# An fp32 kernel of two transformer blocks: the place of the first additions of each part, the size of the weight sums, and the first attention blocks behind a feed-forward layer

## The chip, the cores and the metric

The kernel runs on one core of one Trainium2 chip. The time is device microseconds of the slowest core, here the only one. The kernel before takes 1590.38 us, the median of three runs (1589.19 to 1590.43).

## The reference

A sequence of 512 tokens of width 1,024 in float32 goes through two blocks. The second has two layers, and the change lies in it: the feed-forward layers, and the attention between them (the first block and the first layer's mixer are left out here).

```python
def squared_relu_mlp(n, w_up, w_down):          # w_up 1024 x 4096, w_down 4096 x 1024
    return jnp.square(jax.nn.relu(n @ w_up)) @ w_down

def mixer_c(n, w_in, gq, gk, w_out):            # 8 heads of 128
    q, k, v = _split(n @ w_in, (C_WIDTH, C_WIDTH, C_WIDTH))
    q = rmsnorm_2(q.reshape(bsz, s_len, N_HEADS_C, HEAD_DIM), gq)
    k = rmsnorm_2(k.reshape(bsz, s_len, N_HEADS_C, HEAD_DIM), gk)
    return stick_breaking(q, k, v).reshape(bsz, s_len, C_WIDTH) @ w_out

# stick_breaking, for every head, z = q @ k.T / sqrt(128), only keys before the token:
#   lo = log_sigmoid(-z);  rc = cumsum of lo from the right
#   a = exp(log_sigmoid(z) + rc - lo);  out = a @ v

for layer in range(2):
    n = rmsnorm_2(h, g_mix[layer])
    h = h + (mixer_ab(n, ...) if layer == 0 else mixer_c(n, ...))
    h = h + squared_relu_mlp(rmsnorm_2(h, g_ffn[layer]), w_up[layer], w_down[layer])
```

## The kernel before, in words

**Arithmetic.** Float32 products are made of three matmuls on a high part and a remainder of each operand (`three`, L612 to L614): high x high, remainder x high, high x remainder. A tile of weights has 128 partitions x 2,048 columns (1 MB; eight chunks of the contraction by 256 output columns). SyncE issues its DMA into one of two buffers `raw`, ScalarE copies it rounded into `wh` (the high part), and VectorE subtracts that from `raw` into `wl` (the remainder). The activations are split in the same way. Each engine's order is written out by hand, in one function for each engine; semaphores join them.

**Projection blocks.** A block is 8 chunks x 3 matmuls that fill one PSUM bank. Two banks, G0 and G1, take the blocks in turn, so a block can begin only when the one two before it has been copied out (`take_block`). The other six banks are C0, C1, C2, AV, ST and SX.

**A feed-forward layer** (`layer(f)` in each engine's function) has four parts. A part makes 8 up blocks into `wide` (relu, square, on VectorE L2913 and ScalarE), and multiplies them by its share of `w_down` in seven products of half the size instead of eight, on sums of quarters. The sums of quarters of the weights are GpSimd's: `weight_sum` (L2073), four in a part (t3 = b22 - b12, b12 = b12 - b11, b11 = b22 - b12, b21 = b21 - b11), each in two halves of four pieces of 256 columns; a semaphore is raised after each half. GpSimd also makes the sums of quarters of the values, `pair_sums` (L2078). The last weight sum of a part waits for VectorE's second remainder of product 1 (`half_lo`).

**A product** (`product`, L1222; its matmuls are L1231 to L1233) is four chunks x two banks x three matmuls. Products 0, 2, 4 and 6 use banks C0 and C1, 3 and 5 use C2 and AV, and 1 uses ST and SX. For each, ScalarE rounds the weight quarter in two halves, and VectorE makes two remainders of 1,024 columns (`half_of(i, a)`, L2876). VectorE also adds the finished banks to the accumulator in `wide` (`add_up`, L2896), two instructions for each product, and makes the remainders of pairs of values (`second_pair`, L2876 with 128x512). Since products 0 and 2 share their banks, TensorE waits ahead of product 2 for `acc_added` of product 0, and inside it for the remainders of the last pair of values and of the weights. VectorE's order there is: half_of(1, 0), half_of(1, 1), second_pair(3), half_of(2, 0), add_up(0), half_of(2, 1).

**The end of the first feed-forward layer.** After its last product the sums are transposed (`turn_back`, eight times four transposes, L1259) into banks of the list `BACK` and added to h (`final_add`, L2866). h is then rounded and its remainder formed, chunk by chunk (`feed` on ScalarE, L1395 and L1401; `low` on VectorE, L2232), while GpSimd adds up the squares (`add_squares`, L1955) and splits the sum (L2138). TensorE sums that over the partitions (`norm_stat(4)`, L677 and L678), and ScalarE and VectorE form the root (`rsqrt`, L1379 to L1381; `newton`, L2201 and L2202).

**The attention of the second layer** (`attention_group("stick", g, ...)`) has four groups of two heads. A group projects six blocks from three weight tiles: 0 to 3 (query and key of both heads), 4 and 5 (values). Each of 0 to 3 is squared and summed over the partitions (`head_stat`, the same L677 and L678) for its own norm. TensorE does the scores (`do_scores`, L698), the running sums and turns of the weights (`do_turns`, L712) and their products of the heads of the group before between the blocks of the group at hand; ScalarE and VectorE form the weights (`weights`). In the first group nothing is left of a group before. There blocks 0 and 1 are made side by side, chunk by chunk (`first_stick_blocks`), since the chunks of h come one after another, with the last four `turn_back` after the second chunk; then comes `norm_stat(4)`, then blocks 2 and 3, each of which needs a G bank that was copied out with the norm's root.

## Time and profile before

| | before |
|---|---|
| median of three runs | 1590.38 us (1589.19 to 1590.43) |
| the profiled execution, its own time | 1590.34 us |
| its span | 1588.5 us |
| ScalarE busy | 726.9 us, 46% |
| DMA, mean over the span | 91 GB/s, queue 1 at 26.4% of 16 engines |
| up projections, first line L612, 816 matmuls of 128x512 | 326.1 us, 400 ns each |
| remainders of weights, L2876, 102 of 128x1024 | 172.9 us, 1,707 ns each |

The span is the time from the first to the last instruction; 1.8 us of the profiled time lie around it. Busy times say how much of the span an engine worked; engines run beside each other. The duration of a matmul includes its way through the pipeline: one begins some 0.23 us after the one before, while each lasts 0.39. GB/s and clock are given over the span in 40 slices, and TensorE's granted clock is in the highest tenth in each of them.

### The profile page before, as it was taken

The numbers are of one execution on the slowest core, as the hardware profiler recorded it, in microseconds if no ns is written. First come the engines' busy times: TensorE is split into PE (matmuls) and PEld (weight loads), VectorE is DVE, ScalarE is ACT, GpSimd is POOL, SyncE is SP. The second block draws the span as 40 slices with busy tenths as digits, with TensorE's granted clock in tenths as the row PEclk, the third lists the DMA queues.
The fourth block names the chain that finished last, engine by engine and source line by source line (L and its number), as shares of the span: only waits on it lengthen the run. The fifth ranks groups of instructions, "written<-read, shape, count | busy, mean of one in ns | idle before, by whom it ended". The sixth has DMA issues, their size and how long they took to land.

```text
span 1588.5 us, 20549 instructions
## 1 busy us (share of the span) xinstructions
PE 1562.5 (98%) x7570; PEld 1280.4 (81%) x7570; DVE 1033.2 (65%) x1343; ACT 726.9 (46%) x1084; POOL 672.2 (42%) x666
## 2 busy tenths in 40 slices
PE   9999999999999999999999999899999999999999
PEld 7888787887778898888888888688886888888887
DVE  7424554675678977458484848868777557575847
ACT  6323423324245655434343435567765453444433
POOL 0002120114346443385656657423333484847574
PEclk9999999999999999999999999999999999999999
DMA  7232222232211221323233231222121314141321
GB/s 244 80 106 80 79 79 79 95 106 89 98 53 57 91 79 55 132 80 130 83 106 106 85 128 30 77 80 80 54 80 40 146 53 159 53 159 54 135 78 54
DMA packets 25731, 145.07 MB, mean 91 GB/s; under 512 B 3936, under 2 KB 5680, under 8 KB 9264
## 3 DMA queue, kind: packets, MB, share of 16 engines
q1 hardware_dynamic: 25648, 143.95, 26.4%
q8 instruction: 53, 0.87, 0.2%
q14 instruction: 30, 0.25, 0.1%
HBM read 141.84 MB, written 2.10 MB: 91 GB/s over the span
## 4 chain that ended last, share of the span: by engine, by line
PE 76%; POOL 11%; DVE 9%; ACT 2%; issue 2%; DVEq 0%; ACTq 0%; POOLq 0%
PE ps_G L612 17%; PE ps_G L614 17%; PE ps_G L613 17%; POOL wide L2078 4%; PE ps_C L1231 4%; PE ps_C L1233 4%; PE ps_C L1232 4%; POOL tabs L2073 2%; POOL raw L2073 2%; POOL mixed_buffers L2078 1%; PE ps_C L698 1%; PE ps_AV L1074 1%; PE ps_AV L1232 1%; PE ps_AV L1233 1%; PE ps_AV L1231 1%
## 5 line engine op out<-in xcount | busy, mean ns | idle before, releaser
L612 PE MATMUL ps_G<-ch,wh 128*128 128x512 f32 x816 | 326.1, 400 | 1.7 <-DVE cl L2232 1.6
L613 PE MATMUL ps_G<-cl,wh 128*128 128x512 f32 x816 | 318.4, 390 | 0.0
L614 PE MATMUL ps_G<-ch,wl 128*128 128x512 f32 x816 | 318.3, 390 | 0.0
L612 PE MATMUL ps_G<-nh,wh 128*128 128x512 f32 x504 | 199.7, 396 | 0.4 <-DVE h L2440 0.2
L614 PE MATMUL ps_G<-nh,wl 128*128 128x512 f32 x504 | 196.3, 390 | 0.0
L613 PE MATMUL ps_G<-nl,wh 128*128 128x512 f32 x504 | 196.2, 389 | 0.0
L2876 DVE TENSOR_TENSOR wl<-raw,wh 128x1024 fp32r<-128x1024 f32 (+1 forms) x102 | 172.9, 1707 | 33.2 <-ACT wh L1837 25.1
L612 PEld LDWEIGHTS ps_G<-ch,wh 128*128 128x128 f32 x816 | 153.6, 188 | 42.4 <-issue 7.4
L613 PEld LDWEIGHTS ps_G<-cl,wh 128*128 128x128 f32 x816 | 153.7, 188 | 34.0 <-issue 3.1
L614 PEld LDWEIGHTS ps_G<-ch,wl 128*128 128x128 f32 x816 | 153.6, 188 | 32.4
L2167 DVE TENSOR_TENSOR wl<-raw,wh 128x2048 fp32r<-128x2048 f32 x46 | 107.4, 2334 | 65.2 <-ACT wh L1357 62.1
L1357 ACT ACTIVATE wh<-raw 128x2048 fp32r<-128x2048 f32 x60 | 114.4, 1907 | 69.8 <-PE ps_G L614 69.8
L1881 ACT ACTIVATE wide<-tmp 128x512 f32<-128x512 f32 x64 | 40.5, 632 | 219.1 <-DVE tmp L2913 219.0
L1231 PE MATMUL ps_C<-wh,nh 128*128 128x512 f32 x320 | 125.6, 392 | 4.7 <-DVE wide L2896 4.7
L1233 PE MATMUL ps_C<-wh,nl 128*128 128x512 f32 x320 | 124.6, 389 | 0.0
L1232 PE MATMUL ps_C<-wl,nh 128*128 128x512 f32 x320 | 124.6, 389 | 0.0
L2876 DVE TENSOR_TENSOR nl<-wide,nh 128x512 fp32r<-128x512 f32 (+1 forms) x80 | 68.7, 866 | 85.3 <-ACT nh L1885 46.5
L612 PE MATMUL ps_G<-wh,ch 128*128 128x256 f32 (+1 forms) x400 | 119.1, 298 | 0.0
L614 PE MATMUL ps_G<-wh,cl 128*128 128x256 f32 (+1 forms) x400 | 115.6, 289 | 0.0
L613 PE MATMUL ps_G<-wl,ch 128*128 128x256 f32 (+1 forms) x400 | 115.5, 289 | 0.0
L612 PEld LDWEIGHTS ps_G<-nh,wh 128*128 128x128 f32 x504 | 94.6, 188 | 25.3 <-issue 5.5
L614 PEld LDWEIGHTS ps_G<-nh,wl 128*128 128x128 f32 x504 | 94.6, 188 | 20.1
(426 smaller groups left out, 3150.0 us busy)
## 6 DMA issues: line engine op xcount, KB each, us to landing
raw<-wst SPq DMA_DIRECT2D x96, 1024.0 KB, 5.0
raw<-quart_d SPq DMA_DIRECT2D x16, 1024.0 KB, 4.9
tabs<-quart_d SPq DMA_DIRECT2D x8, 1024.0 KB, 6.9
mixed_buffers<-quart_d SPq DMA_DIRECT2D x8, 1024.0 KB, 5.1
raw<-wst SPq DMA_DIRECT2D x8, 256.0 KB, 6.3
out<-wide SPq DMA_DIRECT2D x8, 256.0 KB, 2.0
h<-xT SPq DMA_DIRECT2D x7, 256.0 KB, 6.5
raw<-wst SPq DMA_DIRECT2D x2, 512.0 KB, 5.5
```

What stands on the lines that cost most here:

```text
L612: mm(o, ah, bh, start=first, stop=False)
L613: mm(o, ah, bl, start=False, stop=False)
L614: return mm(o, al, bh, start=False, stop=last)
L1231: mm(o, ah, bh[:, c, :], start=fresh and c == 0, stop=False, skip_group_check=True)
L1232: mm(o, ah, bl[:, c, :], start=False, stop=False, skip_group_check=True)
L1233: return mm(o, al, bh[:, c, :], start=False, stop=c == 3, skip_group_check=True)
L1357: A(wh[s][:], raw[s][:], ACT.Copy).then_inc(w_hi, 1)
L1881: A(wide[:, k, :], tmp[:, k % 2, :], ACT.Square).then_inc(hid_set, 1)
L2073: ins = g.tensor_tensor(dst[:, w], x[:, w], y[:, w], ALU.subtract)
L2078: g.tensor_tensor(dst, x, y, op).then_inc(value_sums, 1)
L2167: v.tensor_tensor(wl[s][:], raw[s][:], wh[s][:].bitcast(F), ALU.subtract).then_inc(w_lo, 1)
L2876: return tt(lo, x, hi.bitcast(F), ALU.subtract)
```

## The change

Three things change.

First, in every part of both feed-forward layers VectorE adds product 0 to the accumulator (`add_up(0)`) right after the two weight remainders of product 1, ahead of the pair's remainder and the first remainder of product 2, behind which it stood.

Second, `weight_sum` on GpSimd makes each half with one instruction of 1,024 columns instead of four of 256. The semaphore is raised as often as before.

Third, the way from the first feed-forward layer into the attention. ScalarE and VectorE make the high part and the remainder of the second weight tile of the attention already within the end of the layer, between the chunks of h. TensorE works on four blocks: 0 and 1 in the G banks as before, 2 and 3 in banks C0 and C1 (`EARLY`), all on the chunks that are there; the eight turn_back use C2, AV, SX and ST twice. `norm_stat(4)` stands behind chunk 5 of blocks 0 and 1, and the rest of the four blocks comes behind it. The first group's order on ScalarE and VectorE is rewritten to this, blocks 4 and 5 take over the G banks from blocks 2 and 3's places in the count (`after=k - 2`), and the row sum of block 3 (`head_stat`) moves into the second group, behind the scores and block 0.

```diff
@@ end of the first feed-forward layer, TensorE
-        BACK = ("C2", "AV", "SX", "ST", "C0", "C1", "C2", "AV")
+        BACK = ("C2", "AV", "SX", "ST", "C2", "AV", "SX", "ST")
+        EARLY = {2: "C0", 3: "C1"}
...
+                st, end = Step("stick", 0), Part(0, 3)
+                def some(blocks, chunks):
+                    for c in chunks:
+                        pe.wait_ge(n_lo, 8 * LO_OF[4] + c + 1)
+                        for k in blocks:
+                            o, s, col = ps[EARLY.get(k, f"G{st.bank(k)}")], st.slot(k // 2), k % 2 * P
+                            ins = three(o[:], wh[s][:, c, col:col + P], wl[s][:, c, col:col + P], mh[:, c, :], ml[:, c, :],
+                                        c == 0, c == KC - 1)
+                            if c == KC - 1:
+                                give_block(ins, st, k)
                 need_tile(st, 0)
-                for c in range(KC):
-                    pe.wait_ge(n_lo, 8 * LO_OF[4] + c + 1)
-                    for k in range(2):
-                        project_some(st, k, mh, ml, [c], c == 0, c == KC - 1)
-                    if c == 1:
-                        pe.wait_ge(acc_added, Part(0, 3).added(6))
-                        for f in range(4, KC):
-                            pe.wait_ge(h_new, f - 3)
-                            turn_back(f, BACK[f])
+                take_block(st, 0)
+                take_block(st, 1)
+                some((0, 1), range(3))
+                pe.wait_ge(acc_added, end.added(6))
+                for f in range(4, KC):
+                    pe.wait_ge(h_new, f - 3)
+                    turn_back(f, BACK[f])
+                need_tile(st, 1)
+                some((2, 3), range(3))
+                some((0, 1, 2, 3), (3,))
+                some((0, 1), (4, 5))
                 norm_stat(4)
+                some((0, 1), (6, 7))
+                some((2, 3), range(4, KC))
@@ attention_group, TensorE
+                if name == "stick" and g == 1:
+                    stands(pe, before, 2)
+                    stands(pe, before, 3)
...
-                if blocks01 is not None:
-                    blocks01()
-                else:
-                    block_(0, 0, 0)
-                    block_(1, 0, P)
+                if first_blocks is not None:
+                    first_blocks()
+                    head_stat(("qk", qk0))
+                    block_(4, 2, 0)
+                    head_stat(("qk", qk0 + 1))
+                    block_(5, 2, P)
+                    head_stat(("qk", qk0 + 2))
+                    return
+                block_(0, 0, 0)
+                if name == "stick" and g == 1:
+                    head_stat(("qk", qk0 - 1))
+                block_(1, 0, P)
@@ attention_group, ScalarE, the first group of four
+                if g == 0:
+                    rsqrt(("norm", 4))
+                    evac_qk(0, 0)
+                    evac_qk(1, 1)
+                    split(st, 1)
+                    rsqrt(("qk", qk0))
+                    act.wait_ge(rt_set, 2)
+                    evac_qk(2, 2)
+                    values_out(wide[:, 12, :], st, 4, 0)
+                    rsqrt(("qk", qk0 + 1))
+                    split(st, 2)
+                    evac_qk(3, 3)
+                    rsqrt(("qk", qk0 + 2))
+                    values_out(wide[:, 13, :], st, 5, 1)
+                    rsqrt(("qk", qk0 + 3))
+                    return
@@ end of the first feed-forward layer, ScalarE, behind feed(4, c, c % 2)
+                    if c == 1:
+                        act.wait_ge(raw_full[1 - t % 2], st.tile_use(5) * 16 + 16)
+                        free(6, 0)
+                        A(wh[1 - s][:, 0:4, :], raw[1 - t % 2][:, 0:4, :], ACT.Copy).then_inc(second_hi, 1)
+                    if c == 2:
+                        free(6, 1)
+                        A(wh[1 - s][:, 4:8, :], raw[1 - t % 2][:, 4:8, :], ACT.Copy).then_inc(w_hi, 1)
@@ layer(f), GpSimd
-                            for n in range(4 * a, 4 * a + 4):
-                                w = slice(n * TW, (n + 1) * TW)
-                                ins = g.tensor_tensor(dst[:, w], x[:, w], y[:, w], ALU.subtract)
-                            ins.then_inc(weight_sums, 1)
+                            w = slice(1024 * a, 1024 * (a + 1))
+                            g.tensor_tensor(dst[:, w], x[:, w], y[:, w], ALU.subtract).then_inc(weight_sums, 1)
@@ attention_group, VectorE, the first group of four, behind the root's diagonals
+                    split(st, 1)
+                    apply(0, lambda: token_scales(2))
+                    apply(1)
+                    split(st, 2)
+                    apply(2)
+                    apply(3)
+                    return
@@ layer(f), VectorE
                     half_of(1, 0)
                     half_of(1, 1)
+                    add_up(0, X, 0, 0)
                     second_pair(3)
                     half_of(2, 0)
-                    add_up(0, X, 0, 0)
                     half_of(2, 1)
@@ end of the first feed-forward layer, VectorE
                 final_add(3)
-                for c in range(2, KC):
+                low(4, 2)
+                dve.wait_ge(second_hi, 1)
+                subtract(wh[1 - s][:, 0:4, :], wl[1 - s][:, 0:4, :], raw[1 - t % 2][:, 0:4, :])
+                dve.wait_ge(w_hi, t + 2)
+                subtract(wh[1 - s][:, 4:8, :], wl[1 - s][:, 4:8, :], raw[1 - t % 2][:, 4:8, :]).then_inc(w_lo, 1)
+                low(4, 3)
+                final_add(4)
+                final_add(5)
+                for c in range(4, KC):
+                    low(4, c)
                     if c + 2 < KC:
                         final_add(c + 2)
-                    low(4, c)
```

In the order of instructions three places show it. VectorE between products 0 and 2 of the first part, before (`wl<-raw,wh` are remainders of weights, `nl<-wide,nh` those of the last pair of values, `wide<-wide,ps_C` the two additions):

```order
L2923 CAST ones_r<-ones 128x128
L2876 TENSOR_TENSOR wl<-raw,wh 128x1024 x2
L2876 TENSOR_TENSOR nl<-wide,nh 128x2x256
L2876 TENSOR_TENSOR wl<-raw,wh 128x1024
L2896 TENSOR_TENSOR wide<-wide,ps_C 128x512 x2
L2876 TENSOR_TENSOR wl<-raw,wh 128x1024
```

The same place now, with its lines 47 further down:

```order
L2970 CAST ones_r<-ones 128x128
L2923 TENSOR_TENSOR wl<-raw,wh 128x1024 x2
L2943 TENSOR_TENSOR wide<-wide,ps_C 128x512 x2
L2923 TENSOR_TENSOR nl<-wide,nh 128x2x256
L2923 TENSOR_TENSOR wl<-raw,wh 128x1024 x2
L2923 TENSOR_TENSOR nl<-mixed_buffers,nh 128x1024
```

The additions moved ahead of the pair's remainder and of both remainders of product 2. GpSimd in the same stretch, before (the third weight sum of a part, the pair sums, the fourth weight sum, then the first of the next part):

```order
L2073 TENSOR_TENSOR raw<-mixed_buffers,tabs 128x256 x8
L2078 TENSOR_TENSOR mixed_buffers<-wide 128x256
L2078 TENSOR_TENSOR wide<-wide 128x256
L2078 TENSOR_TENSOR wide<-mixed_buffers,wide 128x256
L2078 TENSOR_TENSOR wide<-wide 128x256
L2073 TENSOR_TENSOR raw<-raw 128x256 x8
L2073 TENSOR_TENSOR mixed_buffers<-mixed_buffers,tabs 128x256 x8
```

And now:

```order
L2119 TENSOR_TENSOR raw<-mixed_buffers,tabs 128x1024 x2
L2123 TENSOR_TENSOR mixed_buffers<-wide 128x256
L2123 TENSOR_TENSOR wide<-wide 128x256
L2123 TENSOR_TENSOR wide<-mixed_buffers,wide 128x256
L2123 TENSOR_TENSOR wide<-wide 128x256
L2119 TENSOR_TENSOR raw<-raw 128x1024 x2
L2119 TENSOR_TENSOR mixed_buffers<-mixed_buffers,tabs 128x1024 x2
```

The order is the same, with two instructions for eight. TensorE where the first attention group ends and the second begins, before (`ps_ST<-nh,ones_r` and `ps_ST<-nl,ones_r` are the row sum of block 3, `ps_C<-wide` scores):

```order
L613 MATMUL ps_G<-wl,ch 128x256
L614 MATMUL ps_G<-wh,cl 128x256
L677 MATMUL ps_ST<-nh,ones_r 128x512
L678 MATMUL ps_ST<-nl,ones_r 128x512
L698 MATMUL ps_C<-wide 128x128
L698 MATMUL ps_C<-wide 128x256
L698 MATMUL ps_C<-wide 128x384
L698 MATMUL ps_C<-wide 128x512
L612 MATMUL ps_G<-ch,wh 128x512
```

Now that row sum stands one block later, between the last matmuls of the second group's block 0 and the first of its block 1:

```order
L613 MATMUL ps_G<-ch,wh 128x512
L614 MATMUL ps_G<-cl,wh 128x512
L615 MATMUL ps_G<-ch,wl 128x512
L678 MATMUL ps_ST<-nh,ones_r 128x512
L679 MATMUL ps_ST<-nl,ones_r 128x512
L613 MATMUL ps_G<-ch,wh 128x512
```

The scores and 24 matmuls of a block moved ahead of it; what stands ahead of the scores is now the row sum of block 2.

## Rows read from the trace of the kernel before

**Rows 1.** The page, busy time of each engine, share of the span, instructions.
```profile
PE 1562.5 (98%) x7570; PEld 1280.4 (81%) x7570; DVE 1033.2 (65%) x1343; ACT 726.9 (46%) x1084; POOL 672.2 (42%) x666
```
**Rows 2.** Waits of TensorE by pair: waiting line, releaser, total us, times, longest us.
```profile
PE ps_ST L677 <- POOL nl L2138: 6.2, 1, 6.2
PE ps_C L1231 <- DVE wide L2896: 4.7, 6, 0.8
...
PE ps_G L612 <- DVE cl L2232: 1.6, 4, 0.9
```
**Rows 3.** Timeline of TensorE, product 1 to 2 (start, length, line; idle before, releaser).
```profile
807.32 0.39 PE L1232 MATMUL ps_SX<-wl,nh 128*128 128x512 f32 x1
807.54 0.39 PE L1233 MATMUL ps_SX<-wh,nl 128*128 128x512 f32 x1
808.71 0.50 PE L1231 MATMUL ps_C<-wh,nh 128*128 128x512 f32 x1 [0.78 <-DVE wide L2896]
```
**Rows 4.** Timeline of VectorE, the same place.
```profile
800.36 3.44 DVE L2876 TENSOR_TENSOR wl<-raw,wh 128x1024 fp32r<-128x1024 f32 x2
805.09 0.69 DVE L2876 TENSOR_TENSOR nl<-wide,nh 128x512 fp32r<-128x512 f32 x1 [1.30 <-ACT nh L1855]
806.04 1.42 DVE L2876 TENSOR_TENSOR wl<-raw,wh 128x1024 fp32r<-128x1024 f32 x1 [0.26 <-ACT wh L1846]
807.39 1.27 DVE L2896 TENSOR_TENSOR wide<-wide,ps_C 128x512 f32<-128x512 f32 x2
808.69 1.23 DVE L2876 TENSOR_TENSOR wl<-raw,wh 128x1024 fp32r<-128x1024 f32 x1
```
**Rows 5.** Timeline of GpSimd, the same place: pieces of the last weight sum.
```profile
805.17 7.03 POOL L2073 TENSOR_TENSOR raw<-raw 128x256 f32<-128x256 f32 x5
```
**Rows 6.** Timelines of GpSimd and VectorE, lengths alone and beside each other.
```profile
796.35 2.83 POOL L2073 TENSOR_TENSOR raw<-mixed_buffers,tabs 128x256 f32<-128x256 f32 x4
...
811.52 1.75 DVE L2876 TENSOR_TENSOR wl<-mixed_buffers,wh 128x1024 fp32r<-128x1024 f32 x1
...
1006.93 1.28 POOL L1955 TENSOR_TENSOR fb<-fb,sq 128x512 f32<-128x512 f32 x1 [0.82 <-ACT sq L1401]
...
1001.05 0.75 DVE L2232 SCALAR_TENSOR_TENSOR cl<-h,par,ch 128x512 fp32r<-128x512 f32 x1 [0.21 <-ACT ch L1395]
...
1007.46 1.30 DVE L2232 SCALAR_TENSOR_TENSOR cl<-h,par,ch 128x512 fp32r<-128x512 f32 x1
```
**Rows 7.** Timelines of VectorE and TensorE, first part, products 1 and 2.
```profile
718.49 3.45 DVE L2876 TENSOR_TENSOR wl<-raw,wh 128x1024 fp32r<-128x1024 f32 x2
...
720.36 0.47 PE L1231 MATMUL ps_ST<-wh,nh 128*128 128x512 f32 x1 [0.43 <-issue]
...
726.02 0.50 PE L1231 MATMUL ps_C<-wh,nh 128*128 128x512 f32 x1
```
**Rows 8.** Timelines of three engines behind the first layer's norm.
```profile
676.79 5.83 POOL L2073 TENSOR_TENSOR mixed_buffers<-mixed_buffers,tabs 128x256 f32<-128x256 f32 x7
...
679.52 1.12 DVE L2202 SCALAR_TENSOR_TENSOR tmp<-tmp 128x512 f32<-128x512 f32 x1
...
681.57 0.47 PE L612 MATMUL ps_G<-ch,wh 128*128 128x512 f32 x1 [0.19 <-DVE tmp L2913]
```
**Rows 9.** A wait, and the window behind it: length, PE, PEld, DVE, ACT, POOL, PEclk, DMA, GB/s.
```profile
PE ps_ST L1057 <- DVE tmp L2733: 2.0, 1, 2.0
...
551.00:560.00 9.00, 8.45 (x59) 8.48 (x60) 8.66 (x25) 2.89 (x8) 5.61 (x8) 0.81 0.21 86
```
**Rows 10.** Timeline of TensorE: last product, norm's sum, row sum of block 3.
```profile
1003.07 0.39 PE L1233 MATMUL ps_C<-wh,nl 128*128 128x512 f32 x1
...
1025.87 0.77 PE L677 MATMUL ps_ST<-nh,ones_r 128*128 128x512 f32 x1 [6.15 <-POOL nl L2138]
...
1052.37 0.40 PE L677 MATMUL ps_ST<-nh,ones_r 128*128 128x512 f32 x1
```
**Rows 11.** Timeline of TensorE: the first turns of the weights.
```profile
1067.32 1.44 PE L712 MATMUL ps_C<-small,mixed_buffers 128*128 128x128 f32 x10 [0.79 <-DVE mixed_buffers L2767]
```

More of the change, by code:

```diff
@@ L247, in build @@
         s1_hi, s1_lo, s4_hi, s4_lo = (sem(n) for n in ("s1_hi", "s1_lo", "s4_hi", "s4_lo"))
-        next_hi, acc_clear, acc_added = sem("next_hi"), sem("acc_clear"), sem("acc_added")
+        second_hi, next_hi, acc_clear, acc_added = sem("second_hi"), sem("next_hi"), sem("acc_clear"), sem("acc_added")
         y_turned, h_new, h_turned, acc_from_h = (sem(n) for n in ("y_turned", "h_new", "h_turned", "acc_from_h"))
@@ L598, in take, with take_block @@
                 passed(pe, moved[b], n)
-            def take_block(st, k):
-                passed(pe, moved[f"G{st.bank(k)}"], st.block_use(k))
+            def take_block(st, k, after=None):
+                passed(pe, moved[f"G{st.bank(k)}"], st.block_use(k if after is None else after))
                 return ps[f"G{st.bank(k)}"]
@@ L636, in project_some, with project_v @@
                     give_block(ins, st, k)
-            def project_v(st, k, tile, half, xh=mh, xl=ml, each=None):
-                o = take_block(st, k)
+            def project_v(st, k, tile, half, xh=mh, xl=ml, each=None, after=None):
+                o = take_block(st, k, after)
                 s = st.slot(tile)
@@ L1021, in third, with attention_group @@
                 return ins
-            def attention_group(name, g, hd, prev, qk0, need, set_at=0, blocks01=None, ahead=None):
+            def attention_group(name, g, hd, prev, qk0, need, set_at=0, first_blocks=None, ahead=None):
                 st = Step(name, g)
@@ L1035, in block_ @@
                     else:
-                        project_v(st, k, tile, k % 2, each=last_stats if name == "dsa" and g == k == 0 else None)
+                        project_v(st, k, tile, k % 2, each=last_stats if name == "dsa" and g == k == 0 else None,
+                                  after=k - 2 if name == "stick" and g == 0 else None)
                 def last_stats(c):
@@ L1361, in ready_block, with copy_out @@
                 return ps[f"G{st.bank(k)}"]
-            def copy_out(dst, st, k, scale=1.0, src=lambda o: o[:]):
+            def copy_out(dst, st, k, scale=1.0, src=lambda o: o[:], bank=None):
                 o = ready_block(st, k)
+                o = o if bank is None else ps[bank]
                 A(dst, src(o), ACT.Copy, scale=scale).then_inc(moved[f"G{st.bank(k)}"], 1)
@@ L1656, in evac_qk @@
                         act.wait_ge(st_applied, STAT[("qk", qk0 + n - 2)] + 1)
-                    copy_out(tmp[:, n % 2, :], st, k)
+                    copy_out(tmp[:, n % 2, :], st, k, bank=EARLY.get(k) if name == "stick" and g == 0 else None)
                     stands(act, st, k)
@@ L1789, in attention_group @@
                     return
+                if g == 0:
[14 more added lines that the diff above has]
+                    return
                 split(st, 0)
-                if name == "stick" and g == 0:
-                    rsqrt(("norm", 4))
                 if prev is not None:
@@ L1802, in attention_group @@
                 split(st, 1)
-                if name == "stick" and g == 0:
-                    act.wait_ge(rt_set, 2)
                 evac_qk(2, 2)
@@ L1933, in layer @@
                     feed(4, c, c % 2)
-                free(6, 1)
+                    if c == 1:
[5 more added lines that the diff above has]
+                        A(wh[1 - s][:, 4:8, :], raw[1 - t % 2][:, 4:8, :], ACT.Copy).then_inc(w_hi, 1)
             layer(0)
@@ L2790, in attention_group @@
                 choose = select if soft and g == 0 else lambda *rounds: None
-                if not soft:
+                if not soft and g:
                     split(st, 0)
@@ L2842, in attention_group @@
                     return
-                apply(0, (lambda: token_scales(2)) if prev is None else lambda: None)
-                if prev is None:
-                    split_part(st, 1, 0)
-                    apply(1, lambda: split_part(st, 1, 1))
-                else:
-                    split(st, 1)
-                    apply(1)
-                if prev is not None:
-                    output(prev)
-                    weights(prev + 1)
+                apply(0)
+                split(st, 1)
+                apply(1)
+                output(prev)
+                weights(prev + 1)
                 split(st, 2)
                 apply(2)
-                apply(3, (lambda: output(prev + 1)) if prev is not None else lambda: None)
+                apply(3, lambda: output(prev + 1))
             for g in range(2):
```

1 line of the change is left out of this document (removed).

## The prediction

> **What bounds the kernel.** I read the busy times first: TensorE is busy for 98% of the span [rows 1], so nothing but its waits, some 26 us, can be won, and nothing that other engines do costs time unless TensorE comes to wait for it. Then the waits by pair [rows 2]. Two families concern the change: 6 waits of 0.8 us, 4.7 in all, of product matmuls for VectorE's additions, and in the first attention group behind the first layer one wait of 6.2 us for GpSimd's remainder of the squares, with four small ones of 1.6 us. Then the timelines around them.
>
> The six are alike, one in each part but the first of both layers. At 807.54 TensorE starts the last matmul of product 1, and could start product 2 one spacing of 0.23 (from 807.32 to it) later, at 807.77; it starts at 808.71 [rows 3]. Each wait thus costs 0.94. VectorE's order [rows 4] is: two remainders of weights, the remainder of the last pair of values, one remainder for product 2, then the two additions (1.27), and these end last.
>
> Behind them stands GpSimd. From 805.17 it works on its last weight sum in pieces of 256 columns [rows 5]. VectorE and GpSimd get in each other's way: a remainder of 1,024 columns takes 1.23 alone [rows 4] and 1.75 when a piece of 256 is in its way [rows 6], 0.52 more, out of the piece's 0.71 (2.83 for 4). An instruction of VectorE of 0.75 that starts at 1007.46 under a GpSimd piece of 512 (1006.93, 1.28 long) takes 1.30: it stood until the piece was all but done [rows 6]. So the one that comes second stands for nearly the whole of the other's instruction, and whoever waits is next: the remainders of 1.75 follow each other and each time one piece goes between. The additions read one operand from PSUM and don't take part: 0.64 each, under the pieces too [rows 4].
>
> **First additions sooner.** No work is added. The additions would begin at 803.8, where the two remainders end (800.36 and 3.44), and product 0 has long ended; they end at 805.1. The pair's remainder and the one for product 2 follow, 0.69 and about 1.3: with pieces of 256, they would end at 807.4 and the wait would be gone, 6 x 0.94 = 5.6 us. That is the term the reordering would bring alone.
>
> **Weight sums by 1,024.** Four pieces become one. From 256 (0.71) and 512 (1.28) columns, 0.57 for each 256 more, a piece of 1,024 takes 0.71 + 3 x 0.57 = 2.42 and stands in VectorE's way for all but 0.2 of it, 2.2. GpSimd saves 0.4 of 2.8 us on each half sum, and nobody waits for these sums in the rows: worth nothing. But VectorE, the busiest helper in the products, meets it at the worst place. The last weight sum waits only for VectorE's second remainder of product 1 (803.4 to 803.8) and for GpSimd's own pair sums, which now come about a microsecond sooner, since the sum ahead of them is shorter. I let its first piece begin at 804.0. VectorE adds until 805.1, stands until 806.2, forms the pair's remainder until 806.8; the second piece, waiting, goes next, until 809.0; only then the remainder for product 2, until 810.15. TensorE could have begun at 807.77, and begins 1.5 later than before. Ends of this term: 0.9 less than before if nothing gets in the way; 0.4 more if the first piece begins after the pair's remainder (at 805.17 as now: 805.8 + 2.2 + 1.15, the 1.23 less its overlap with the next, = 809.15); 1.6 more at the most. I take 1.5, because the pieces' start follows from order and sizes. 6 x 1.5 = 9.0.
>
> The first part of both layers starts product 2 with hardly a wait now, in the first layer at 726.02 [rows 7]. There VectorE is done with product 1's remainders at 721.94; the first piece goes from 721.6 or so to 723.8, the pair's remainder to 724.4, the second piece to 726.6, product 2's remainder to 727.7: 1.7 later, and 1.9 in the second layer by the same working. 3.6 for both; the 0.4 wait ahead of product 1 at 720.36 may go, which I leave in the bounds.
>
> One more place: behind the first layer's norm, GpSimd's first weight sum starts at 676.79 while VectorE forms the root [rows 8]. The second step of the root, which ends at 680.64 now, would stand under the second piece until 681.9 and end at 682.6; TensorE's third block, held until 681.57 by the copy behind it, starts 1.9 later. In the second layer the same shift is inside 1 us of slack. Elsewhere in the parts a whole up block of 24 matmuls, 5.4 us, covers VectorE's tile remainders, and nothing is lost while that cover stands.
>
> The Trainium skill, page SBUF — State Buffer, section Who interferes with whom, speaks against this part too: a VectorE instruction with two SBUF inputs and a GpSimd one that reads SBUF exclude each other, for the whole instruction of whichever was first. The 512-column row agrees; no row here shows 1,024. GPSIMD Engine Reference, section 3.1, gives 4,497 ns for a two-input operation of 2,048 fp32 columns; a piece of 1,024 would be 2.3 by that, as an estimate, and the sum 2 us smaller.
>
> **The clock.** The clock fell to half (1.2 of 2.4 GHz) behind a wait of 2.0 us ahead of L1057: granted 0.81 over the 9 us behind it, which costs 9 x 0.19 = 1.7 us of matmuls [rows 9]. Behind the six waits of 0.8 it stayed up (their matmuls follow at 0.23). The nine new waits are of 1.9 to 2.4. I price half of them: 4.5 x 1.7 = 7.6; ends 0 and 15.
>
> **Four blocks side by side.** The 6.2 us wait is at 1025.87 [rows 10]: both G banks hold finished blocks, and TensorE has nothing left. Now four blocks are in work when the norm's sum is formed, and the row sum of block 3 (its head statistic) comes behind the scores and block 0 of the next group. The stretch from the last product's end (1003.3) to that row sum at 1052.37 is 49.1 us [rows 10], of which 6.2 + 1.6 + 0.3 are waits and some 3 slow matmuls and restarts behind them. 38.0 of work remain; scores and a block, now ahead of it, add 7.2 (1.8 from the rows' starts, and 24 matmuls at 0.227). New waits: 0.6 at chunk 2, because VectorE's third low part now stands behind its additions and one more; and 1.4 ahead of block 4, whose weight remainder VectorE forms only behind the root's diagonals. Sum 47.2: the row sum falls at 1050.2, 2.2 sooner, with seven microseconds of TensorE's work more behind it.
>
> That lead is not kept. What comes next on ScalarE is unchanged: the root of block 3, the copy of the next tile (1.9 long), then the weights of the next heads; VectorE and GpSimd follow in their order. From the row sum at 1052.37 to the turns of the weights at 1067.32 the chain takes 14.95 us [rows 11], and TensorE's own work between was 13.5; it now has only block 1 and a row sum, 6 us, left to cover it. So it waits about 9 us there, in two pieces, and the net gain is the 2.2 of the chain. The clock would fall in that wait as it did in the 6.2 one, and cost about 1.7. I take a gain of 0.5, ends 2.2 gained and 2 lost (if the clock falls at block 4 too).
>
> **Sum.** 9.0 + 3.6 + 1.9 + 7.6 - 0.5 = +21.6. The profiled execution took 1590.34 (span 1588.5), the median is 1590.38. Forecast 1612.
>
> **Rivals.**
> - *Nothing stands between* (0.17). GpSimd lets VectorE in before its second piece, or inside a long one. For it: no row shows 1,024 columns. Against it: in every pair of rows the waiting engine goes next. 5.6 gained, 0.4 at 720.36, 0.5 behind the layer: 1584. This is the other side; it decides at whether product 2's remainder ends before 807.77.
> - *Only one piece stands in the way* (0.13). The sum's first piece begins after the pair's remainder, as now. 6 x 0.4 + 3.6 + 1.9 - 0.5, with waits of about 1.4 that leave the clock up: +7.4, 1598. For it: GpSimd's pair sums may stand longer under the remainders than I let them.
> - *The lead behind the layer is kept* (0.04), with the additions: 5.6 and 9 gained, 1576. Against it the 14.95 us of chain.
> - *It comes to nothing* (0.04): smaller holds and the six additions cancel, 1588 to 1593.
>
> Forecast 0.62, its own range 1600 to 1619: from no fallen clock to nearly all. For 8 in 10 the range must take in the first two rivals: 1583 to 1619. Faster by over 0.2% (3.2 us, what a measurement of this kernel can tell): 0.17 + 0.04 = 0.21. Within: 0.04. Slower: 0.13 + 0.62 = 0.75.
>
> **What would show it.** GpSimd's pieces of 2.4 us, and of 3.5 where they stood; VectorE's remainders of 1,024 columns at up to 3.4 instead of 1.75; a wait of 2 to 2.5 ahead of product 2 in all eight parts, for a remainder and no more for an addition; granted clock 0.5 behind some; a wait near 7 us ahead of the first row sum of the second group, none of 6 behind the norm. Wrong it would be if the remainders never exceed 1.8, or if product 2 starts at once.

## The result

The changed kernel takes 1618.07 us (median of four runs, 1617.46 to 1618.62) against 1590.41 before on the same chip: a ratio of 1.0175, 95% interval 1.0163 to 1.0187. It is 27.7 us slower. The forecast was 1612, its range 1583 to 1619, slower with a chance of 0.75; the result lies 0.9 under the range's upper end.

**The profile after.** The page's first part, which answers to [rows 1]:

```profile
PE 1571.6 (97%) x7570; PEld 1288.1 (80%) x7570; DVE 1053.4 (65%) x1343; ACT 727.4 (45%) x1085; POOL 589.2 (36%) x474
```

VectorE works 20 us more with the same 1,343 instructions, and most of that is time for which it stood: with pieces of 256 in the changed kernel it works 1036.5. GpSimd works 83 us less. The 0.4 that I gave for each of 64 half sums makes 26 of them; the short pieces had stood behind VectorE too, five of them 7.03 us in [rows 5], where five alone take 3.5. TensorE has the same 7,570 matmuls in 9 us more, since some of them ran at half clock. TensorE's waits by pair, to be read beside [rows 2]:

```profile
PE ps_C L1243 <- issue: 18.9, 8, 2.6
PE ps_ST L678 <- POOL nl L2183: 6.9, 1, 6.9
PE ps_G L613 <- DVE wl L2212: 2.5, 1, 2.5
PE ps_G L613 <- DVE tmp L2960: 2.1, 1, 2.1
...
PE ps_G L613 <- DVE cl L2277: 0.5, 1, 0.5
```

Six waits of 0.8 for an addition became eight of 2.3 to 2.6 (L1243 is the first matmul of each chunk of a product; "issue" says that the profile names no releaser; VectorE's timeline gives it below). A wait of 2.1 behind the first norm's root is new. The wait of 6.2 in the attention has moved one group on and is 6.9 now.

The same place as [rows 3] to [rows 5], in the second part. TensorE, then VectorE, then GpSimd:

```profile
812.48 0.39 PE L1245 MATMUL ps_SX<-wh,nl 128*128 128x512 f32 x1
815.21 0.47 PE L1243 MATMUL ps_C<-wh,nh 128*128 128x512 f32 x1 [2.34 <-issue]
```

```profile
808.19 1.27 DVE L2943 TENSOR_TENSOR wide<-wide,ps_C 128x512 f32<-128x512 f32 x2
809.50 2.29 DVE L2923 TENSOR_TENSOR nl<-wide,nh 128x512 fp32r<-128x512 f32 x1
811.72 4.52 DVE L2923 TENSOR_TENSOR wl<-raw,wh 128x1024 fp32r<-128x1024 f32 x2
816.16 1.21 DVE L2923 TENSOR_TENSOR nl<-mixed_buffers,nh 128x1024 fp32r<-128x1024 f32 x1
```

```profile
808.83 5.19 POOL L2119 TENSOR_TENSOR raw<-raw 128x1024 f32<-128x1024 f32 x2
```

The additions end at 809.46, sooner than TensorE needs them, and they run at 0.64 each, the second of them under GpSimd's piece: they read PSUM. The two pieces one by one:

```profile
808.83 2.41 POOL L2119 TENSOR_TENSOR raw<-raw 128x1024 f32<-128x1024 f32 x1
811.21 2.82 POOL L2119 TENSOR_TENSOR raw<-raw 128x1024 f32<-128x1024 f32 x1
```

The pair's remainder, 0.69 alone, takes 2.29, since it stands until the first piece ends at 811.24. The second piece takes 2.82 instead of 2.41, since it stands behind that remainder. The first of the two remainders takes 3.4 of the 4.52, since the second piece went first. It ends at 815.1, and product 2 starts at 815.21, 2.5 later than one spacing behind 812.48.

Behind the first layer's norm the same shows on the root's two steps; the second took 1.12 before [rows 8] and takes 2.75 now:

```profile
676.38 5.18 POOL L2119 TENSOR_TENSOR mixed_buffers<-mixed_buffers,tabs 128x1024 f32<-128x1024 f32 x2
```

```profile
677.95 1.38 DVE L2246 SCALAR_TENSOR_TENSOR tmp<-tmp 128x512 f32<-128x512 f32 x1 [2.03 <-ACT tmp L1410]
679.36 2.75 DVE L2247 SCALAR_TENSOR_TENSOR tmp<-tmp 128x512 f32<-128x512 f32 x1
```

The clock, in windows behind two of the eight waits (columns as in [rows 9]) and in the attention's wait:

```profile
815.00:820.00 5.00, 4.79 (x14) 3.83 (x15) 4.65 (x5) 0.18 (x1) 0.00 (x0) 0.66 0.50 175
...
1499.00:1504.00 5.00, 4.74 (x21) 3.97 (x22) 5.00 (x6) 1.06 (x1) 0.00 (x0) 1.00 0.55 177
...
1075.50:1085.50 10.00, 5.62 (x18) 4.48 (x19) 6.80 (x10) 6.63 (x13) 5.17 (x5) 0.50 0.24 95
```

Behind seven of the eight waits the granted clock was 0.66 over 5 us or 0.72 over 6; at 1499 alone it stayed at 1.00. In the attention it was 0.50, which is 1.2 of 2.4 GHz, for the whole 10 us.

**Where the 27.2 us of span are.** Starts of the same instruction in both traces give them by stretch. From the first product of the first layer to its first turn_back: 284.5 before and 297.1 now, 12.6 more. In the second layer, from its first product to the last one's end, 11.5 more. The two are 24.1, of which the later starts of product 2 are 13.8 (1.56 in each of six parts, 1.9 and 2.5 in the first ones) and the slow matmuls the other 10.3, about 1.5 for each of the seven. Ahead of the first product 1.5 more: the wait behind the norm is 1.9 longer, and 0.4 had been gained between 552 and 580, where the change touches nothing (below). From the first turn_back to the first turns of the weights 0.3 less, and from there to the next group's turns 2.0 more, at half clock. All later groups take the same time as before.

### The profile page after: what moved, and what is told of

It reads as the page before. It is cut to its first block, busy times and chain, and to the rows that moved or that the text cites. A ratio compares the mean times of both kernels' runs of the same rounds, so it can differ in the third digit from the quotient of the medians.

```text
span 1615.7 us, 20359 instructions
## 1 busy us (share of the span) xinstructions
PE 1571.6 (97%) x7570; PEld 1288.1 (80%) x7570; DVE 1053.4 (65%) x1343; ACT 727.4 (45%) x1085; POOL 589.2 (36%) x474
## 4 chain that ended last, share of the span: by engine, by line
PE 86%; DVE 10%; issue 2%; ACT 2%; POOL 0%; DVEq 0%; ACTq 0%; POOLq 0%
PE ps_G L613 19%; PE ps_G L614 19%; PE ps_G L615 19%; PE ps_C L1243 5%; PE ps_C L1244 5%; PE ps_C L1245 5%; DVE wide L2617 1%; DVE top L2613 1%; PE ps_C L699 1%; PE ps_AV L1076 1%; PE ps_AV L1243 1%; PE ps_AV L1245 1%; PE ps_AV L1244 1%; PE ps_C L713 1%; DVE wide L2807 1%
## 5 line engine op out<-in xcount | busy, mean ns | idle before, releaser
L613 PE MATMUL ps_G<-ch,wh 128*128 128x512 f32 x800 | 319.8, 400 | 2.6 <-DVE tmp L2960 2.1
L614 PE MATMUL ps_G<-cl,wh 128*128 128x512 f32 x800 | 312.0, 390 | 0.0
L615 PE MATMUL ps_G<-ch,wl 128*128 128x512 f32 x800 | 311.9, 390 | 0.0
L2923 DVE TENSOR_TENSOR wl<-raw,wh 128x1024 fp32r<-128x1024 f32 (+1 forms) x104 | 187.8, 1824 | 37.6 <-ACT wh L1878 25.4
L1243 PE MATMUL ps_C<-wh,nh 128*128 128x512 f32 x320 | 129.9, 406 | 18.9 <-issue 18.9
L2923 DVE TENSOR_TENSOR nl<-wide,nh 128x512 fp32r<-128x512 f32 (+1 forms) x80 | 90.5, 1140 | 77.7 <-ACT nh L1926 46.5
L1244 PE MATMUL ps_C<-wl,nh 128*128 128x512 f32 x320 | 128.7, 402 | 0.0
L1245 PE MATMUL ps_C<-wh,nl 128*128 128x512 f32 x320 | 128.6, 402 | 0.0
L613 PEld LDWEIGHTS ps_G<-nh,wh 128*128 128x128 f32 x504 | 94.6, 188 | 25.6 <-issue 5.5
L614 PEld LDWEIGHTS ps_G<-nl,wh 128*128 128x128 f32 x504 | 94.7, 188 | 19.9 <-issue 1.0
```

Of the source, the lines that this page charges most:

```text
L613: mm(o, ah, bh, start=first, stop=False)
L614: mm(o, ah, bl, start=False, stop=False)
L615: return mm(o, al, bh, start=False, stop=last)
L1243: mm(o, ah, bh[:, c, :], start=fresh and c == 0, stop=False, skip_group_check=True)
L1244: mm(o, ah, bl[:, c, :], start=False, stop=False, skip_group_check=True)
L1245: return mm(o, al, bh[:, c, :], start=False, stop=c == 3, skip_group_check=True)
```

## The experiments

The first five take the change apart. Kernels are compared with the kernel before on the same chip.

**Pieces of 256 again, the rest as changed.**

```diff
-                            w = slice(1024 * a, 1024 * (a + 1))
-                            g.tensor_tensor(dst[:, w], x[:, w], y[:, w], ALU.subtract).then_inc(weight_sums, 1)
+                            for n in range(4 * a, 4 * a + 4):
+                                w = slice(n * TW, (n + 1) * TW)
+                                ins = g.tensor_tensor(dst[:, w], x[:, w], y[:, w], ALU.subtract)
+                            ins.then_inc(weight_sums, 1)
```

> The changed kernel with its weight sums in four pieces of 256 columns again; additions and attention blocks as changed. My theory (the long pieces do the harm, the two other edits are sound or nearly neutral): the waits ahead of product 2 are gone in all eight parts, the clock falls in none of them, and the wait behind the first layer's norm is gone. 5.7 (six waits) and 0.6 (the one ahead of the first product 1) gained on the kernel before, and some 1.4 given back at the attention, where the trace of the changed kernel shows a wait of 6.9 and a fallen clock: 1586, between 1583 and 1589. Rival A (the moved additions do the harm, since they put three remainders into the way of the last weight sum whatever its pieces): over 1600, with waits of 1 or more ahead of product 2. Rival B (the attention part costs most of it): over 1600 with no wait ahead of product 2.

Measured 1586.50 against 1590.47, ratio 0.9976 (0.9967 to 0.9985). No product waits but the first product 1 (0.4), and the clock fell in no part. With the short pieces the change would have been a small gain: the 31.6 us between these two kernels come with the longer pieces. Both rivals fall.

**Nothing but the pieces of 1,024.**

> The kernel before with nothing changed but the weight sums in pieces of 1,024 columns. My theory: VectorE's order there is the pair's remainder, one remainder, the additions, so two pieces stand in its way ahead of the additions, and product 2 waits for these about 3.7 instead of 0.94, in six parts (+16.5), 2.8 in the two first ones (+5.5), 2 behind the norm, and the clock falls behind most of the nine (up to 15): 1622 to 1630, slower than the whole change, which has the additions out of the way. Rival A (the moved additions are at fault): 1590 to 1597.

Measured 1597.73 against 1590.47, ratio 1.0046 (1.0031 to 1.0062): slower, but by 24 to 32 less than I expected. The waits ahead of product 2 are there in all eight parts and short:

```profile
PE ps_C L1231 <- DVE wide L2894: 9.4, 8, 1.4
```

VectorE and GpSimd in its second part show why:

```profile
805.71 1.23 DVE L2874 TENSOR_TENSOR nl<-wide,nh 128x512 fp32r<-128x512 f32 x1
806.86 3.42 DVE L2874 TENSOR_TENSOR wl<-raw,wh 128x1024 fp32r<-128x1024 f32 x1
810.21 1.27 DVE L2894 TENSOR_TENSOR wide<-wide,ps_C 128x512 f32<-128x512 f32 x2
811.51 2.09 DVE L2874 TENSOR_TENSOR wl<-raw,wh 128x1024 fp32r<-128x1024 f32 x1
```

```profile
806.35 6.17 POOL L2072 TENSOR_TENSOR raw<-raw 128x1024 f32<-128x1024 f32 x2
```

I had let the first piece begin ahead of the pair's remainder. It begins behind it, and only one piece stands in front of the additions (the remainder of 3.42). The second, whose turn comes at 810.2, when that remainder is done, runs beside the additions, which it doesn't hold, and is over but for 0.9 when the next remainder comes. No clock fell behind these waits of 1.2 to 1.4.

**Nothing but the additions first.**

> The kernel before with nothing changed but the first additions ahead of the pair's remainder. My theory: TensorE doesn't wait ahead of product 2 in any part, 5.7 gained, and the trace's other waits stay: 1584.7, between 1583.5 and 1586.5. Rival A: slower than before.

Measured 1583.13 against 1590.47, ratio 0.9953 (0.994 to 0.9967): 7.3 gained. The interval, 5.2 to 9.5, holds the 5.6 of the six waits, and these are gone from the trace.

**Both, without the attention part.** It was run later, once the two parts were known to be worth -7.3 and +7.3 alone.

> The kernel before with the additions first and the weight sums by 1,024, without the attention part. Alone, the additions gained 7 and the sums lost 7, so without an effect of one on the other: 1590. My theory (the additions, which read PSUM, hid the second piece; moved ahead of the sum they no longer do, and both pieces stand in the way): waits of 2.5 ahead of product 2 in all parts and a fallen clock behind most, 1612 to 1618.

Measured 1615.94 against 1590.37, ratio 1.0165 (1.0149 to 1.018). Together the two cost 25.6, though their effects alone add up to nothing:

```profile
PE ps_C L1231 <- issue: 18.9, 8, 2.5
```

This is what the change did. At their old place the additions hid the sum's second piece. At the new one they cover only the first 0.6 of its first piece, and the waits grow from 1.2 to 1.4 us to 2.3 to 2.5. The clock fell behind five of these eight in the execution profiled here, behind seven of eight in the change's, and behind none of the shorter ones.

**Nothing but the attention part** (four blocks side by side, their order on all engines, the second tile early).

> The kernel before with the attention part of the change alone (four blocks side by side, the second tile made early, the row sum of block 3 one block later), sums by 256 and additions at their old place. My theory: the lead is given back ahead of the turns of the weights. The way from the last product to those turns is as long as before or up to 1 shorter, and the clock, which falls in the new wait of 6.9, costs up to 3 more behind it: 1589 to 1593, that is no gain. Rival B (it costs most of the 27 us): over 1600. Rival C (it gains by itself, and only the long pieces or the fallen clock hid that): 1583 to 1587, since the waits of 6.2 and 1.6 would be gone.

Measured 1593.17 against 1590.47, ratio 1.0018 (1.0009 to 1.0027): 2.7 lost (1.4 to 4.3 by the interval), 0.2 past the end of my range and no gain in any case. The first turns of the weights start 68.2 us behind the first turn_back, where it was 68.5, and 2 us follow at half clock. Rivals B and C fall.

**Pieces of 512, and sums in one instruction of 2,048.** The edit is the slice's width.

> The changed kernel with pieces of 512 columns. My theory: a piece holds VectorE for 1.1; one stands ahead of the pair's remainder and one ahead of product 2's first remainder, the third ahead of the second, which isn't late. Waits ahead of product 2 of 0.3 to 0.9, so that the clock stays up; behind the norm 0.7: 1593, between 1589 and 1597. Rival (a threshold in the length: anything over 256 is as bad as 1,024): 1610 or more.

> The changed kernel with every weight sum in one instruction of 2,048 columns. My theory (the engines take turns, and whoever comes second stands for the whole of the other's instruction): now one piece of twice the hold stands ahead of the pair's remainder and none behind it, so product 2 begins where it does now, with a wait of 2.5; the norm's root stands once, for as long: 1614 to 1622, no difference from the change. Rival (the longer the piece the longer each wait, whatever the number): waits of 4 or more, 1632 or more. Rival (a long instruction lets VectorE in by and by): waits under 1.5, under 1605.

By 512: 1590.77 against 1590.39, ratio 1.0002 (0.9992 to 1.0011). By 2,048: 1636.09, ratio 1.0284 (1.0269 to 1.03). Their waits, 512 first:

```profile
PE ps_C L1243 <- issue: 1.5, 8, 0.4
PE ps_G L613 <- DVE tmp L2962: 1.1, 1, 1.1
```

```profile
PE ps_C L1243 <- issue: 21.9, 8, 2.8
PE ps_C L1243 <- DVE nl L2921: 9.7, 8, 1.6
PE ps_ST L678 <- POOL nl L2181: 6.9, 1, 6.9
PE ps_G L613 <- DVE tmp L2958: 3.9, 2, 2.2
```

```profile
814.48 4.49 DVE L2921 TENSOR_TENSOR nl<-wide,nh 128x512 fp32r<-128x512 f32 x1
818.90 2.35 DVE L2921 TENSOR_TENSOR wl<-raw,wh 128x1024 fp32r<-128x1024 f32 x2
```

```profile
813.82 4.61 POOL L2117 TENSOR_TENSOR raw<-raw 128x2048 f32<-128x2048 f32 x1
```

There is no threshold at 256. Ahead of product 2 the taking of turns holds: one piece of 4.61 ahead of the pair's remainder and none behind it makes waits of 2.6 to 2.8, about what two pieces made (2.3 to 2.6), and pieces of 512 leave 0.2 to 0.4. The total of the 2,048 I missed, by 14 to 22 us: a third family appears, eight waits of 0.2 to 1.6 inside product 0, ahead of its last chunk, for the last remainder of the first pairs of values (L2921, `nl`). The piece of the sum before holds VectorE there for 3.1 (a remainder of 0.69 takes 3.83); two pieces, between which VectorE gets its turn, had held it for 0.9 (799.28, 1.62 in the changed kernel's trace) and made no wait. A longer piece also costs at places where the shorter one had slack.

**The last weight sum later, pieces of 1,024 kept.**

```diff
-                    pool.wait_ge(half_lo, pt.half(1, 1))
+                    pool.wait_ge(half_lo, pt.half(3, 1))
```

> The changed kernel, pieces of 1,024, but the last weight sum of a part waits for VectorE's remainders of product 3 instead of product 1. Nothing else differs. My theory (two long pieces of that one sum stand in front of the pair's remainder and of product 2's): no wait ahead of product 2, no fallen clock there; at its new place VectorE is ahead by more than the 4.4 that the two pieces hold it. The 2.1 behind the first norm stays. 1590.5 - 5.7 - 0.6 + 2.1 + 2.7 (the attention part as measured by itself) = 1589, between 1586 and 1592. Rival (the sum can't be put anywhere without a wait, since VectorE is busy for most of the products): the wait appears ahead of product 3 or 4 with 1 to 2.5, 1600 or more. Rival (the long pieces cost through all four sums): 1605 or more.

Measured 1587.32 against 1590.39, ratio 0.998 (0.9971 to 0.9989). One number in one wait takes back 31 us. No product waits at all, not even the first product 1, and no clock fell in a part. The pieces still hold VectorE at their new place, where a remainder alone takes 1.22:

```profile
812.25 2.71 DVE L2923 TENSOR_TENSOR wl<-tabs,wh 128x1024 fp32r<-128x1024 f32 x1 [0.85 <-ACT wh L1887]
814.88 1.27 DVE L2943 TENSOR_TENSOR wide<-wide,ps_C 128x512 f32<-128x512 f32 x2
816.18 2.13 DVE L2923 TENSOR_TENSOR wl<-tabs,wh 128x1024 fp32r<-128x1024 f32 x1
```

TensorE doesn't come to wait for it. The long pieces are harmless where VectorE is ahead; of the four sums only the last one did harm in the parts.

**Another order at the start of the second attention group.** Pieces of 256. ScalarE, with VectorE and TensorE to match (mean of block 3, first half of the weights, root, second half, tile's remainder; the row sum behind chunk 1 of the next block):

```diff
+                if g == 1:
+                    softplus(prev, HALVES[0])
+                    rsqrt(("qk", qk0 - 1))
+                    softplus(prev, HALVES[1])
+                    evac_qk(0, 0)
+                    split(st, 0)
```

> Pieces of 256 (as in the first run of this study, 1586.5) with another order at the start of the second attention group: the row sum of block 3 after two chunks of its block 0; ScalarE makes the first half of the first head's weights ahead of the root of block 3 and the second half ahead of the copy of the next tile; VectorE likewise, with the tile's remainder last. My theory (the lead is lost only because these chains stand one behind the other): the wait of 6.9 ahead of the next row sum shrinks to under 1, the turns of the weights come 5 to 8 sooner, the clock doesn't fall there for 10 us: 1574 to 1579. Rival (the chain has no slack, its sum is bound by VectorE's own work): the wait moves to the turns with 5 or more, 1584 to 1587.

Measured 1580.18 against 1590.39, ratio 0.9935 (0.9922 to 0.9949), 6.3 faster than with the order of the change. TensorE there:

```profile
1047.60 0.66 PE L678 MATMUL ps_ST<-nh,ones_r 128*128 128x512 f32 x1 [2.42 <-DVE cols L2269]
...
1059.30 0.40 PE L678 MATMUL ps_ST<-nh,ones_r 128*128 128x512 f32 x1
1059.54 0.39 PE L679 MATMUL ps_ST<-nl,ones_r 128*128 128x512 f32 x1
1059.77 1.28 PE L713 MATMUL ps_C<-small,mixed_buffers 128*128 128x128 f32 x10
1061.73 0.50 PE L613 MATMUL ps_G<-ch,wh 128*128 128x512 f32 x1 [0.68 <-DVE wl L2221]
```

The wait of 6.9 is gone and the turns follow at once; in its place stand 2.4 at the row sum that I put forward (for VectorE's root of block 2, with a fallen clock of 0.66 over 5 us behind it) and 0.7. The turns begin 64.0 behind the first turn_back, where it was 68.2 in the change: 4.2 sooner, not the 5 to 8 that I expected. My theory was right about the cause, and the time is 1 to 6 longer than I expected.

**Two attempts at what was left.**

> As the run with the other order at the start of the second attention group (1580.2), and two things more. The row sum of block 3 goes behind chunk 5 of the next block instead of chunk 1, where it waited 2.4 for VectorE. ScalarE copies that group's next tile ahead of the root of block 2, and VectorE forms its remainder while ScalarE works on that root (idle 2.0 there), not behind the weights. My theory (the rest of the lead hangs on VectorE, busy without a gap for 12.9 from block 3's mean to the tile's remainder): the wait of 2.4 and the low clock behind it (1.7) go, block 2 of the group starts 2 sooner than 1061.7: 1575 to 1578. Rival (the squares' remainder on GpSimd bounds it): a wait of 2 to 3 ahead of the next row sum takes the place, 1578 to 1581.

> As the run before, and the tile of blocks 4 and 5 sooner: ScalarE copies it ahead of block 1's copy, VectorE forms its remainder ahead of the root's diagonals. My theory: the wait of 2.5 ahead of block 4 goes, but the row sum behind block 4 waits for block 0's root instead, which VectorE ends as late as before, so that 1 at most of the 2.5 is won: 1574 to 1577. Rival (no chain behind it): 2.5 and with it the time, 1573.

1583.32 (ratio 0.9956, 0.9942 to 0.9969) and 1582.66 (0.995, 0.9936 to 0.9963) against 1590.37: both slower than the run before, where I had expected 2 to 6 faster. Their intervals overlap with that of 1580.18 (0.9922 to 0.9949), though every single run of the two, 1581.28 or more, is slower than its slowest, 1581.23. So neither gained, and the size of the loss is not sure. The tile's remainder in VectorE's gap met GpSimd's remainder of block 3's squares. VectorE and GpSimd in the first of the two:

```profile
1042.91 2.29 DVE L2221 TENSOR_TENSOR wl<-raw,wh 128x2048 fp32r<-128x2048 f32 x1 [0.33 <-ACT wh L1387]
1045.12 1.78 DVE L2255 SCALAR_TENSOR_TENSOR tmp<-tmp 128x512 f32<-128x512 f32 x1
```

```profile
1042.96 3.40 POOL L2192 TENSOR_TENSOR nl<-sq,nh 128x512 fp32r<-128x512 f32 x1
```

GpSimd's 1.29 became 3.40, then the root's step 0.69 became 1.78, and the turns came at 1060.74 with a wait of 2.05 ahead of them, 65.6 behind the first turn_back instead of 64.0. The gap had not been free: GpSimd was using it. In the second, the wait of 2.5 ahead of block 4 shrank to 0.9, and 0.8 appeared at the row sum behind it, as expected; the time, 0.7 less than the first's, can't be told from it.

**Long pieces, placed.** The two waits below, and the order at the start of the second attention group of the run that took 1580.18.

```diff
+                    if pt.first:
+                        pool.wait_ge(st_applied, STAT[("norm", (3, 5)[f])] + 1)
                     weight_sum(t3, b22, b12)
...
-                    pool.wait_ge(half_lo, pt.half(1, 1))
+                    pool.wait_ge(half_lo, pt.half(3, 1))
```

> The changed kernel with its pieces of 1,024 kept, but placed: the last weight sum of a part waits for the remainders of product 3, the first one of a layer for the end of that norm's root; and the second attention group begins in the order of the run that took 1580.2. My theory (a long piece costs only where VectorE's next SBUF instruction is awaited by TensorE): no wait over 0.7 ahead of any product and none of 2 behind the norm, so the time is that of the same order with pieces of 256, 1578 to 1581. Rival (the long pieces cost a little everywhere): 1583 or more. Rival (the sums that now begin late meet VectorE elsewhere): a new wait of 1 to 2 in a part, 1585 to 1592.

Measured 1578.53 against 1590.73, ratio 0.9922 (0.9908 to 0.9935). Its median is the lowest of this study. It is faster than both kernels, but can't be told from the same order with pieces of 256 (1580.18, 0.9922 to 0.9949). Its waits on the two placed sums' account are gone; those of the attention remain:

```profile
PE ps_G L613 <- DVE wl L2221: 3.2, 2, 2.5
PE ps_ST L678 <- DVE cols L2269: 2.4, 1, 2.4
```

## Why the prediction was right, and where it was off

**Additions first.** Right: -5.6 forecast, -7.3 alone, with 5.6 inside its interval.

**Weight sums by 1,024.** Right in mechanism and size. Product 2 starts 1.56 later in six parts (forecast 1.5) and 1.9 and 2.5 later in the first ones (1.7 and 1.9); 13.8 in all against 12.6. The length of a piece was given as 2.42 and is 2.41 where it didn't stand. The Trainium skill, page SBUF — State Buffer, section Who interferes with whom, says that a VectorE instruction with two SBUF inputs contends with a GpSimd one that reads SBUF, and that the one behind is blocked for the whole of the other. The trace agrees at 1,024 columns, where no row before had shown it: a remainder of 0.69 took 2.29, while additions with a PSUM operand stayed at 0.64. The working rested on a start at 804.0, ahead of the pair's remainder. In the change that holds in kind (GpSimd's piece at 808.83, the additions' end at 809.46). It holds because the additions are first: with the old order the piece begins behind the remainder. That the size came out as near as 1.56 to 1.5 is in part luck: the piece starts 0.56 behind the two remainders (808.27), not 0.2, but these end 4.4 ahead of the moment at which TensorE is free (812.71), not 4.0 as before, and the two nearly cancel. I named the start as the thing that decides, and it did, but had I seen that the additions were the second piece's cover I could have said outright that the two edits cost 25 together and nothing apart.

**Behind the norm.** 1.9 forecast, and the wait grew by 1.9, from 0.19 to 2.1. The block starts only 1.5 later, because the changed kernel's trace was 0.4 ahead before it came there.

**The clock.** The term most off in the parts. I let it fall behind half of nine waits at 1.7 each, 7.6; it fell behind seven of the eight of 2.3 to 2.6 (and not behind the norm's 2.1) at 1.5 each, 10.3. The bounds of 0 and 15 held it. "Half" was a guess, and no run shows what decides it.

**The attention.** The chain of 14.95 us from the row sum of block 3 to the turns was forecast to stay, and took 14.93 (1066.14 to 1081.07). The lead ahead of it was overrated: that row sum comes 0.3 sooner, not 2.2. By my own terms it should have read 1.9 (1003.3 and 47.2 make 1050.5, not 1050.2). The wait ahead of block 4 was 2.5 instead of 1.4, because the tile's remainder stood behind GpSimd's remainder of block 1's squares. VectorE, with the same instruction on the next tile, then GpSimd:

```profile
1042.69 3.26 DVE L2212 TENSOR_TENSOR wl<-raw,wh 128x2048 fp32r<-128x2048 f32 x1
...
1057.42 2.28 DVE L2212 TENSOR_TENSOR wl<-raw,wh 128x2048 fp32r<-128x2048 f32 x1
```

```profile
1042.19 1.61 POOL L2183 TENSOR_TENSOR nl<-sq,nh 128x512 fp32r<-128x512 f32 x1
```

And the clock stayed down for 10 us in the wait of 6.9 instead of the 7 that the 6.2 had cost. So the term is +1.7 instead of -0.5. I had used the rule of turns for the weight sums and not for the squares, where it also held.

**The sum.** 13.8 + 1.5 + 10.3 + 1.7 = 27.3 against 21.6. Of the 5.7 that are missing, the clock is 2.7, the attention 2.2, and the waits 1.2; 0.4 comes off, by which the changed kernel's trace was ahead at the norm. Of the rivals, "nothing stands between" fell with the pair's remainder of 2.29 above; "only one piece stands" is what the long pieces do without the moved additions.

## What to carry to other kernels

Before you make a helper's instructions longer, look at what the other helper has to do next for the engine that bounds, and in which memory its operands lie: one long GpSimd instruction holds up the steps of VectorE with two operands in SBUF that come up meanwhile, and a step that reads one of them from PSUM is cover for it. Two edits of one stretch can be worth -7 and +7 us apart, and +25 together, so they are to be measured together. And if a long piece is wanted, place it by a wait where its neighbour is ahead: one changed constant took back 31 us of the changed kernel here.

## What the runs showed of the hardware

The price of a wait of TensorE isn't in proportion to its length. Eight waits of 1.2 to 1.4 cost their length; of the eight of 2.3 to 2.6, seven (five in another kernel) cost 1.5 more each, since the granted clock was at half behind them; of the eight of 2.6 to 2.8 with pieces of 2,048, five were followed by a fallen clock. Nor does it go with the kernel. Ahead of block 4 of the first attention group one and the same wait of 2.5 is in nine of the fourteen traces, and the clock fell in it or behind it in three. Ahead of L1057 (L1059 in the changed kernel), which the change doesn't touch, a wait of 2.0 was followed by a fallen clock before [rows 9] and in eleven other traces, and by a granted clock of 1.00 in the changed kernel's and one more. TensorE came out of that stretch 1.5 further ahead, at 555.8, and lost 1.2 of it again at the next turns of the weights, at 580: that is the 0.4 above. So a term of the clock has to be given as a range, and a microsecond or two between two profiled executions can lie in it alone.

And VectorE's exclusion with GpSimd works both ways: GpSimd's remainder of 1.29 took 3.40 behind a VectorE instruction of 2.29.
